# A transformer layer with experts: projections that scale in their high part's pass, sums of squares taken a stage earlier, first weights loaded ahead, and latent norms by token

## The reference

```python
def _rmsnorm(x, g):
    y = xf * lax.rsqrt(jnp.mean(xf * xf, axis=-1, keepdims=True) + EPS)
    return (y * g.astype(jnp.float32)).astype(x.dtype)

    c_q, c_kv, k_r = _split(p, [Q_LORA, KV_LORA, MLA_ROPE])      # 256, 128, 64 columns
    q = (_rmsnorm(c_q, q_norm_g) @ w_uq).reshape(...)
    kv = (_rmsnorm(c_kv, kv_norm_g) @ w_ukv).reshape(...)
    q_nope, q_rope = q[..., :MLA_NOPE], _rope(q[..., MLA_NOPE:], positions)
...
    hn = _rmsnorm(h, norm_mix_g[l])
    p = hn @ w_in[l]
    ...
    h = h + jnp.concatenate([y_mla, y_rwkv], axis=-1) @ w_out[l]
    hn = _rmsnorm(h, norm_xa_g[l])
    memn = _rmsnorm(mem, norm_mem_g[l])
    h = h + _cross_attention(hn, memn, xa_wq[l], xa_wk[l], xa_wv[l], xa_wo[l])
    hn = _rmsnorm(h, norm_ffn_g[l])
    h = h + _peer(hn, peer_wq[l], peer_keys[l], expert_u[l], expert_v[l])
return _rmsnorm(h, final_norm_g)
```

## Time and profile before

| | us |
|---|---|
| median of 3 runs | 4106.72 |
| lowest, highest | 4093.33, 4114.6 |
| the profiled execution, its span | 4113.26, 4111.7 |
| TensorE busy | 3719.7 (90%) |
| VectorE busy | 2736.7 (67%) |
| GpSimd busy | 1947.0 (47%) |
| ScalarE busy | 1249.3 (30%) |

### The profile page before, as it was taken

One profiled execution on the slowest core, in us unless ns is written; L12 is line 12 of the kernel. 1 busy time (PEld: TensorE's weight loads), 2 busy tenths in 40 slices (PEclk: granted clock), 3 DMA queues, 4 the chain that ended last, 5 costly groups with the idle time before them and its releaser, 6 DMA issues.

```text
span 4111.7 us, 54995 instructions
## 1 busy us (share of the span) xinstructions
PE 3719.7 (90%) x19168; PEld 3173.5 (77%) x19168; DVE 2736.7 (67%) x5219; ACT 1249.3 (30%) x1834; POOL 1947.0 (47%) x1352
## 2 busy tenths in 40 slices
PE   6958879999788888999989999999879999899998
PEld 5834468888666576889989899999757888778787
DVE  5453357776304326857778788888698666689896
ACT  2013234333102213133323333333333333333333
POOL 2005022232001001888778888888888888422220
PEclk9979889999989999999999999999999999999999
DMA  2229500000221013548878898888789999899996
GB/s 98 95 92 396 230 24 18 18 9 9 82 92 41 0 41 135 93 83 232 257 230 264 253 266 257 268 260 262 206 224 253 280 279 269 276 370 398 376 401 232
DMA packets 376335, 788.59 MB, mean 192 GB/s; under 512 B 137105, under 2 KB 245649, under 8 KB 342289
## 3 DMA queue, kind: packets, MB, share of 16 engines
q1 hardware_dynamic: 210320, 451.28, 32.6%
q0 software_dynamic: 165888, 336.01, 28.1%
HBM read 643.09 MB, written 144.05 MB: 191 GB/s over the span
## 4 chain that ended last, share of the span: by engine, by line
PE 24%; POOL 18%; DMA 6%; issue 6%; DVE 5%; DVEq 1%; ACT 1%; SPq 1%; POOLq 0%; ACTq 0%
PE peer_ps L2111 15%; POOL gates_d L2000 14%; PE peer_ps L2019 4%; PE peer_ps L2033 4%; DMA late_in<-gates_d 4%; POOL rows L1980 2%; POOL peer_rows L1980 2%; DMA peer_gat<-gates_d 1%; DMA rows<-in_expert_uv,peer_idx 1%; DVEq L2319 1%; PE peer_ps L2057 1%; DMA peer_rows<-in_expert_uv,peer_idx 1%; DVE peer_acc L2404 1%; ACT peer_uh L2203 0%; DVE late_rows L2389 0%
## 5 line engine op out<-in xcount | busy, mean ns | idle before, releaser
L2000 POOL DMA_INDIRECT gates_d<-peer_gates,peer_idx x768 | 1352.4, 1761 | 327.3 <-issue 223.7
L2019 PE MATMUL peer_ps<-high,peer_uh 128*128 128x384 f32 x2048 | 533.4, 341 | 64.7 <-DVE peer_ul L2306 58.6
L2019 PE MATMUL peer_ps<-low,peer_uh 128*128 128x384 f32 x2048 | 528.4, 339 | 0.0
L2019 PE MATMUL peer_ps<-high,peer_ul 128*128 128x384 f32 x2048 | 526.7, 338 | 0.0
L2019 PEld LDWEIGHTS peer_ps<-high,peer_uh 128*128 128x128 f32 x2048 | 373.8, 191 | 77.6 <-issue 70.7
L2019 PEld LDWEIGHTS peer_ps<-low,peer_uh 128*128 128x128 f32 x2048 | 377.3, 191 | 0.0
L2019 PEld LDWEIGHTS peer_ps<-high,peer_ul 128*128 128x128 f32 x2048 | 376.8, 191 | 0.0
L2111 PE MATMUL peer_ps<-peer_vh,peer_ah 128*128 128x512 f32 x1026 | 325.2, 399 | 39.1 <-DVE peer_al L2423 39.1
L1980 POOL DMA_INDIRECT late_rows<-in_expert_uv,peer_idx x108 | 144.3, 1336 | 394.5 <-DVE peer_acc L2404 353.2
L2111 PE MATMUL peer_ps<-peer_vh,peer_al 128*128 128x512 f32 x1026 | 320.7, 394 | 0.0
L2111 PE MATMUL peer_ps<-peer_vl,peer_ah 128*128 128x512 f32 x1026 | 320.1, 394 | 0.0
(11 more groups left out here) (442 smaller groups left out, 7580.5 us busy)
## 6 DMA issues: line engine op xcount, KB each, us to landing
late_in<-in_expert_uv SPq DMA_DIRECT2D x170, 512.0 KB, 5.5
gates_d<-mla_zeros POOLq DMA_DIRECT2D x128, 512.0 KB, 29.6
peer_raw<-in_expert_u SPq DMA_DIRECT2D x128, 512.0 KB
hidden_d<-peer_hid SPq DMA_DIRECT2D x128, 384.0 KB, 3.0
peer_val<-in_expert_uv SPq DMA_DIRECT2D x86, 512.0 KB, 5.0
late_in<-hidden_d SPq DMA_DIRECT2D x170, 192.0 KB, 5.8
late_in<-gates_d SPq DMA_DIRECT2D x170, 192.0 KB, 6.5
peer_act_in<-hidden_d SPq DMA_DIRECT2D x86, 192.0 KB, 5.4
```

The source lines that it names most:

```text
L2000: pool.indirect_dma_start(gates_flat, bass.IndirectOffsetOnAxis(ap=idx[:, n, k:k + 1], axis=0), gates[:, n, k:k + 1], None, compute_op=ALU ...
L2019: last = nc.tensor.matmul(ps[i][:, a, 0:HD], w[:, cols], x[:, kc, a * HD:(a + 1) * HD], start=(kc == 0 and w is uh[i % 2] and x is high), ...
```

## The change

1. The constants' stage also loads x, the positions and the first weights; it squares x, sums the squares in 16 float32 products into PSUM (`x_sums`), and makes the angles and the sine.
2. In projections with a norm ScalarE makes the high part straight from the input with the gain as its scale, and VectorE the low part in one scalar_tensor_tensor. GpSimd's adds and the scaled buffers are gone.
3. The sums of squares for `xq` and `peer` come from the residual stage in front: ScalarE squares tiles 0 to 6 as they are taken, GpSimd adds them (`rstd` holds the partial sum), and the projection only adds the last tile: four float32 products in its second tile. `pin` has its sums already.
4. The first weight tile of every projection lies in `first_raw`, loaded by the stage in front; in `pin` the features are read back for `mprep` too.
5. The latent norms sum squares by token: 24 products with squares as weights and one column of ones give `[128, 16]`. Root and reciprocal are taken of these 16 columns, and a product of the identity with them, multiplied by ones in four float32 products, spreads them to all partitions.

The diff, cut to its core:

```diff
+def build_constants(nc, consts, cols_d, x_d, xT, x_sums, weights, first_raw, positions, ang, sin):
...
+            sp.dma_start(pos_i[:, :], positions.broadcast_to([ROPE, T])).then_inc(pos_loaded, 16)
+            for kc in range(KC):
+                sp.dma_start(xT[:, kc, :], x_d[kc]).then_inc(x_loaded[kc], 16)
+            sp.dma_start(first_raw[:, :], weights[0]).then_inc(raw_loaded, 16)
...
+            for kc in range(KC):
+                act.wait_ge(x_loaded[kc], 16)
+                if kc >= 2:
+                    act.wait_ge(sq_used, kc - 1)
+                nc.scalar.activation(sq[:, kc % 2, :], xT[:, kc, :], ACT.Square).then_inc(sq_ready, 1)
+            act.wait_ge(angle_ready, 1)
+            nc.scalar.activation(sin[:, :], arg[:, :], ACT.Sin)
...
     def highs(self, act, loaded=None):
...
         for kc in range(KC):
             if self.gain:
-                act.wait_ge(self.scaled_ready, kc + 1)
...
-            self.nc.scalar.activation(self.high[:, kc, :], self.part(kc), ACT.Copy).then_inc(self.high_ready, 1)
...
+                self.nc.scalar.activation(self.high[:, kc, :], self.src[:, kc, :], ACT.Copy,
+                                          scale=col(self.consts, self.gain, kc)).then_inc(self.high_ready, 1)
...
+    def sum_squares(self, pe):
+        if self.partial:
+            pe.wait_ge(self.sq_ready, 1)
+            for h in range(2):
+                part = slice(h * HALF, (h + 1) * HALF)
+                self.nc.tensor.matmul(self.sums[:, h, :], self.consts["ones"][:, :], self.rstd[:, part],
+                                      start=True, stop=False)
+                last = self.nc.tensor.matmul(self.sums[:, h, :], self.consts["ones"][:, :], self.sq[:, part],
+                                             start=False, stop=True)
...
+    def lows(self, dve):
+        for kc in range(KC):
+            dve.wait_ge(self.high_ready, kc + 1)
+            if self.gain:
+                self.nc.vector.scalar_tensor_tensor(out=self.low[:, kc, :], in0=self.src[:, kc, :],
+                                                    scalar=col(self.consts, self.gain, kc),
+                                                    in1=self.high[:, kc, :].bitcast(F32), op0=ALU.mult,
+                                                    op1=ALU.subtract).then_inc(self.low_ready, 1)
...
     def first_loads(self, sp):
-        for i in range(2):
-            sp.dma_start(self.raw[i][:, :], self.weights[i]).then_inc(self.w_ready[i], 16)
+
+        sp.nop().then_inc(self.w_ready[0], 16)
+        sp.dma_start(self.raw[1][:, :], self.weights[1]).then_inc(self.w_ready[1], 16)
...
+    def load_following(self, sp):
+
+        if self.following is not None:
+            sp.wait_ge(self.w_low, self.n - 1)
+            sp.dma_start(self.raw[0][:, :], self.following).then_inc(self.next_loaded, 16)
+            sp.wait_ge(self.next_loaded, 16)
...
+            for t in range(NT):
+                tokens = slice(t * P, (t + 1) * P)
+                nc.tensor.matmul(sums[:, t:t + 1], sq[:, 0, tokens], consts["ones"][:, 0:1], start=True, stop=False)
+                nc.tensor.matmul(sums[:, t:t + 1], sq[:, 1, tokens], consts["ones"][:, 0:1], start=False, stop=True)
+                last = nc.tensor.matmul(sums[:, NT + t:NT + t + 1], sq[:, 2, tokens], consts["ones"][:, 0:1],
+                                        start=True, stop=True)
...
+                nc.vector.tensor_tensor(diag[:, part, :], consts["ident"][:, :].unsqueeze(1).broadcast_to([P, NT, P]),
+                                        std[:, part].unsqueeze(2).broadcast_to([P, NT, P]), ALU.mult
+                                        ).then_inc(diag_ready, 1)
...
+        @block.gpsimd
+        def _(pool):
+            pool.nop().then_inc(sq_added, 2)
+            for f in range(1, KC - 1):
+                pool.wait_ge(sq_ready, f + 1)
+                nc.gpsimd.tensor_tensor(partial[:, :], (sq[0] if f == 1 else partial)[:, :], sq[f % 2][:, :],
+                                        ALU.add).then_inc(sq_added, 1)
+                pool.wait_ge(sq_added, f + 2)
...
+            def square(i, tile):
+
+                act.wait_ge(proj.taken, tile + 3)
+                act.wait_ge(sq_added, tile + 1)
...
+                nc.scalar.activation(sq[i][:, :], dst[:, at, :].rearrange("p a t -> p (a t)"),
+                                     ACT.Square).then_inc(sq_ready, 1)
...
-            load_raw(0)
+            sp.nop().then_inc(raw_ready[0], 16)
```

More of the change, by code:

```diff
@@ L296, in sum_squares @@
[L296 to L301, removed]
-                                         start=(m == 0), stop=(m == KC // 2 - 1))
-        last.then_inc(self.sq_summed, 1)
-    def lows(self, dve, loaded=None):
-        for kc in range(KC + 1 if self.gain else KC):
-            if self.gain and kc < KC:
-                if loaded is not None:
-                    dve.wait_ge(loaded[kc], 16)
-                if kc >= 2:
-                    dve.wait_ge(self.high_ready, kc - 1)
-                    dve.drain()
-                self.nc.vector.tensor_scalar(self.scaled[:, kc % 2, :], self.src[:, kc, :],
-                                             col(self.consts, self.gain, kc), None,
-                                             ALU.mult).then_inc(self.scaled_ready, 1)
-            k = kc - 1 if self.gain else kc
-            if k >= 0:
-                dve.wait_ge(self.high_ready, k + 1)
-                if self.gain:
-                    dve.wait_ge(self.scaled_ready, k + 1)
-                self.nc.vector.tensor_tensor(self.low[:, k, :], self.part(k), self.high[:, k, :].bitcast(F32),
-                                             ALU.subtract).then_inc(self.low_ready, 1)
@@ L456, in _ @@
             proj.first_loads(sp)
-            for kc in range(KC):
-                sp.dma_start(xT[:, kc, :], x_d[kc]).then_inc(loaded[kc], 16)
             def store(i, tile):
@@ L558, in _ @@
-            for h in range(2):
-                nc.tensor.matmul(rot_ps[:, h, :], consts["rot"][:, :], kr[:, h * HALF:(h + 1) * HALF],
-                                 start=True, stop=True).then_inc(rot_ready, 1)
-            pe.wait_ge(sq_ready, 3)
-            for f in range(3):
-                for h in range(2):
-                    last = nc.tensor.matmul(sums[:, (f // 2) * 2 + h, :], consts["ones"][:, :],
-                                            sq[:, f, h * HALF:(h + 1) * HALF], start=(f != 1), stop=(f != 0))
@@ new lines, in _ @@
+            last.then_inc(sums_ready, 1)
+            pe.wait_ge(loaded, 16)
+            for h in range(2):
+                last = nc.tensor.matmul(rot_ps[:, h, :], consts["rot"][:, :], kr[:, h * HALF:(h + 1) * HALF],
+                                        start=True, stop=True)
+            last.then_inc(rot_ready, 1)
+            for w in range(2):
+                pe.wait_ge(diag_ready, w + 1)
+                for a in range(2 * w, 2 * w + 2):
+                    last = nc.tensor.matmul(spread[:, a, :], consts["ones"][:, :],
+                                            diag[:, 4 * a:4 * a + 4, :].rearrange("p t c -> p (t c)"),
+                                            start=True, stop=True)
+                last.then_inc(spread_ready, 1)
```

349 lines of the change are left out of this document (177 added, 172 removed).

## The result

The kernel after takes 4047.97 us (median of four runs, 4036.35 to 4056.22), beside 4110.66 (4093.33 to 4119.19) for the one before on the same chip: a ratio of 0.9855, interval 0.983 to 0.988. The forecast was 4036, with 4014 to 4063 around it. The number alone lies nearer to rival A's 4051 than to 4036; it is the stages that tell the two apart. The profiled execution took 4044.39 us, span 4042.7; against the 4113.26 of before that is 68.9 less, where the sum had said 70.9.

A forecast was written before the change was run, and what follows sets the result against it. The prediction took thin stage heads before 1589 us, then a TensorE-bound stretch, as the bound. Terms 7.8 + 15.7 + 19.8 + 13.8 (queries) + 13.8 (experts) = 70.9 us off the median 4106.72 gave 4036, range 4014 to 4063.

The forecast's parts named there:

- rival A: Constants' stage and norms: cold clock eats the new f32 work, front ends at 35 us, total 4051 us; chance 0.15.
- Loads ahead: Five projections: first weights loaded a stage earlier save 3.9 us each, 7.8 us for the two residual ones.
- The front: Constants' stage and input projection: next stage starts at 25.3 us, 9.9 later, yet 15.7 us saved net.
- ScalarE's scale: High parts in normed projections: scaling by a column costs nothing; only beyond 0.4 us more a part would it cost.
- Latent norms: Norms stage: summing by token with features already there takes 24.8 us instead of 44.6, saving 19.8 us.
- Adds beside the projection: Residual stages: GpSimd's adds and ScalarE's squares cost nothing; without cover the adds would cost 31 us.
- the sign of a lost cover: Residual stages: VectorE operations of 2.6 us beside GpSimd's adds would show that the adds block VectorE.
- D: Last stretch: TensorE's granted clock drops below 0.95 and eats the gain, about 4133 us at 0.94; chance 0.04.
- B: Heads or expert stage: part is given back, about half of 71 us, total 4071 us; chance 0.09.
- C: Expert stage: its end is set by something not tied to its start, total 4107 us; chance 0.06.
- One test that the forecast set itself: Last stretch: the prediction is wrong if its length changes by more than 15 us.
- the sum's last step: Whole kernel: 70.9 us taken from the profiled 4113.26 gives 4042.4; taken from the median 4106.72 it gives 4036.

The follow-up runs named there:

- experiment 1: Kernel before with only the latent norms summed and inverted by token, inputs still loaded there: 4101.14 us beside 4104.45, ratio 0.9991; norms stage 35.3 us for 44.6.
- experiment 3: Kernel after with GpSimd's adds in the residual stages cut to 8 columns: ratio 0.9846; output projection 94.6 us for 95.2, second residual 94.9 for 94.9.
- experiment 4: Kernel before with GpSimd's adds in its three normed heads cut to 8 columns: ratio 0.9966; the three stretches 15.7 us shorter together.
- experiment 2: Kernel after with each projection's first weights loaded in its own stage again: ratio 0.9897; the five stages 16.1 us longer together.
- experiments 8 to 12: Unchanged repeat profiles: before, experiment 1, after, a variant with squares added in pairs, before; attention stage 223.2, 233.7, 237.3, 237.5, 237.2 us.
- the second set: Kernel after timed again unchanged against the kernel before: 4042.05 us, ratio 0.9852.

## Why the prediction was right

**Loads ahead.** Forecast 3.9 a projection; the two residual stages gave 3.6 and 3.7, and undoing the loads cost 2.9 to 3.5. The mechanism held, the size was some 15% high.

**The front.** Forecast: the constants' work ends at 24.2 and the next stage starts at 25.3; measured 23.4 and 24.6. The first square came 0.7 us late (7.4 for 6.7), but the cold start cost about 2 us (15.73 less eight pieces of 1.7) where the forecast had left 3.9: rival A (front at 35) fell. Both stages together give 17.5 where 15.7 was said: the third tile starts 14.8 us earlier (13.5 was said; the stage starts 0.7 sooner and the head is 27.1 for 27.6 us), and from there to the end the stage is 2.7 us shorter, where the second cold start that stays away was put at 2.2.

**ScalarE's scale.** Taken at nothing, allowed up to 0.4 us a part; it costs 0.09 (1.05 for 0.96, from 8.42 and the 7.67 of the earlier trace rows). VectorE's low part is 1.21 for 1.15. TensorE's 1.36 stayed last, and the third tiles come 33.4 and 34.4 us after the start for 33.1 and 33.9.

**Latent norms.** 25.1 for 24.8. The choice near the upper end was right for the products: 10.4 us, with two records of 0.21 us each, at half clock. That the loads carry half of the gain (experiment 1) the forecast had in its chain, but not as a term.

**Adds beside the projection.** Cost nothing, as said (experiment 3), and the sign of a lost cover (VectorE operations of 2.6 us) is nowhere: every low part in the two stages takes 1.22 us. The cover was a little better than said: the low part has not only begun but ended when the add starts. What the forecast did not spell out is that in the old heads the adds cost 15.7 us (experiment 4), of the 53 us by which these three stages became shorter (26.7, 13.2 and 13.3); it priced the new heads from TensorE's side and so had that in without naming it. The loads ahead are another 9.4 (experiment 2). If the two prices add up, 28 of the 53 us are left for the shorter passes and for the sums taken a stage earlier, against the 9.2 by which the constants' stage grew; no run prices these apart.

**Rivals.** A fell with the front. D (a lower granted clock in the last stretch) fell: 0.98 as before. B (part given back) fell in the form in which it was put: the heads came out as priced and the last stretch kept its length. A give-back in the attention stage, which B did not name, stays open (experiments 8 to 12). C (the end tied to something else) fell: the last stretch begins 70.7 us earlier (1518.5 for 1589.2) and keeps its length to 1.7 us. One test that the forecast set itself was too sharp: a last stretch off by 15 us would have proved nothing, since the unchanged kernel's moved by 14.9 between two profiles.

**The size of the whole.** The time came out 12 us above the forecast. Of these 3.9 are the kernel before itself, whose median went from 4106.72 to 4110.66 with its fourth run. The other 8.2 are the gain: the run times give 4110.66 - 4047.97 = 62.7 for 70.9, and in the second set, where the kernel after took 4042.05 beside 4103.36, 61.3. In the profiles the stages sum to 69. So the sum's last step, from a profiled execution to the median, which held every unedited stage at its length, is what came out worst, by some 6 us. Over all runs on record, 39 of before (mean 4104.9) and 10 of after (4044.3), the two are 60.6 apart. The three profiles of before lie at 4113, 4111 and 4108, 6 us above that mean, while single runs of it scatter by 8.8 (standard deviation), so this may be the luck of three draws. The attention stage is where old and new heads differ on average (7.6 us). Which of the two is the gap stays open, as runs without a profile don't show their stages.

## What to carry to other kernels

In a chain of stages with barriers price an edit by when it lets the next tile start, and add up engine by engine who is last; the busy shares of the span do not tell it. Work that is moved from a head into a stage where its engine's neighbour idles can be free, and can give back more than it cost in busy time: look at which instructions of another engine grow beside it. To verify edits of under 15 us compare the edited stages in the profiles, since unedited ones move by that much.

## What the runs showed of the hardware

- TensorE's granted clock falls inside a stage in some executions and not in others of the same kernel: 0.92 and 0.98 over the attention stage, 237 and 223 us, with the same work and order. The fall takes some 24 us and comes at one place of a pass of 54 us, in the second, third or fourth pass or not at all. The runs of one kernel spread over 20 us and more; falls like this one may be part of that; no run shows it.
- Of the 24 products with one column each takes 0.43 us from start to start, at a granted clock of 0.50, which is 1.2 GHz; TensorE had idled 10.7 us before them. The weight loads fill that time (10.43 of 10.50 us), and the single column saves little: 0.21 a record, where one of 128 columns took 0.24 in the earlier trace rows. The rotation behind them still ran at 0.50. The windows over the two in the kernel after:

```profile
236.50:247.00 10.50, 10.44 (x49) 10.43 (x49) 3.72 (x4) 0.01 (x2) 0.00 (x0) 0.50 0.00 0
247.00:250.60 3.60, 3.60 (x5) 1.05 (x5) 2.61 (x3) 2.76 (x4) 0.00 (x0) 0.50 0.00 0
```

- A reciprocal takes 12.95 us for 2048 columns, 6.55 for 1024 and 0.25 for 16: its price goes by columns, so a value for each token is inverted best with tokens on the partitions.
